# Retention and banded attention on one Trainium2 core: a gate tile moved inside a head's score blocks, and gate tiles one attention unit sooner

## The reference, cut to what matters

```
q_r, k_r, v_r, g_r, q_a, k_a, v_a, gate_r, gate_a = parts
y_r = retention_branch(q_r, k_r, v_r, g_r, ...) @ w_ret_o     # 8 heads, 64-wide keys, 128-wide values
y_a = attention_branch(q_a, k_a, v_a, ...) @ w_att_o          # 8 heads, band of 128 tokens to each side
mix = (sigmoid(gate_r) * y_r + sigmoid(gate_a) * y_a) @ w_mix_o
```

## Time and profile before

| | |
|---|---|
| median of 3 runs | 4184.95 us (4178.0 to 4199.9) |
| the profiled execution, own time | 4187.68 us |
| its span, first to last instruction | 4185.9 us |
| mean granted clock of TensorE | 0.973 |
| retention stage, layer 0 | about 184 to 345 us |
| attention stage, layer 0 | about 345 to 590 us |
| retention stage, layer 1 | about 1255 to 1412 us |
| attention stage, layer 1 | about 1412 to 1600 us |

### The profile page before, as it was taken

How to read it: one execution, slowest core, us unless ns; L and a number is a source line. 1 busy time by engine, 2 the same in 40 slices (tenths; PEclk the granted TensorE clock), 3 DMA queues, 4 the chain that set the end, 5 groups by cost and what they waited for, 6 DMA issues and landing times. The chain is left out here.

```text
span 4185.9 us, 55886 instructions
## 1 busy us (share of the span) xinstructions
PE 3987.6 (95%) x22458; PEld 3463.1 (83%) x22458; DVE 2238.5 (53%) x3931; ACT 1471.3 (35%) x2120; POOL 838.9 (20%) x763
## 2 busy tenths in 40 slices
PE   8999998999799999899979989899999999999998
PEld 7877798999684567888757887689999998999997
DVE  4333446445433344555547544347997665656664
ACT  3144345222313433522237343333333333333332
POOL 1000013111100001211101430006655563111100
PEclk9999999999998999999989999999999999999999
DMA  3101123222120112322212112226766777887873
GB/s 131 51 31 41 46 86 106 91 86 95 47 71 25 41 50 76 118 101 90 97 46 82 35 57 81 76 91 194 227 198 190 242 254 257 291 266 262 266 246 122
DMA packets 232448, 519.43 MB, mean 124 GB/s; under 512 B 36160, under 2 KB 134592, under 8 KB 231808
## 3 DMA queue, kind: packets, MB, share of 16 engines
q1 hardware_dynamic: 160752, 400.75, 29.1%
q0 software_dynamic: 18432, 67.12, 4.6%
q10 hardware_dynamic: 53008, 47.99, 3.4%
HBM read 454.66 MB, written 60.82 MB: 123 GB/s over the span
## 5 line engine op out<-in xcount | busy, mean ns | idle before, releaser
L304 PE MATMUL PSM<-UX,PARTS 128*128 128x264 f32 (+3 forms) x3392 | 1192.2, 351 | 43.0 <-DVE UX L333 26.3
L305 PE MATMUL PSM<-UX,PARTS 128*128 128x264 f32 (+3 forms) x3392 | 1171.9, 345 | 0.0
L306 PE MATMUL PSM<-UX,PARTS 128*128 128x264 f32 (+3 forms) x3392 | 1168.1, 344 | 0.0
L272 DVE TENSOR_TENSOR PARTS<-RAW,PARTS 128x1024 fp32r<-128x1024 f32 x549 | 687.3, 1258 | 627.1 <-ACT PARTS L262 627.0
L262 ACT ACTIVATE PARTS<-RAW 128x1024 fp32r<-128x1024 f32 x612 | 644.8, 1056 | 991.5 <-PE PSM L306 487.6
L304 PEld LDWEIGHTS PSM<-UX,PARTS 128*128 128x128 f32 x3392 | 651.2, 192 | 133.8 <-DVE UX L333 35.9
L305 PEld LDWEIGHTS PSM<-UX,PARTS 128*128 128x128 f32 x3392 | 651.9, 192 | 60.2 <-issue 3.1
L306 PEld LDWEIGHTS PSM<-UX,PARTS 128*128 128x128 f32 x3392 | 650.8, 192 | 59.7
L2543 PE MATMUL PSM<-AC,PARTS 128*128 128x448 f32 x1024 | 375.3, 367 | 3.8 <-DVE AC L2790 3.8
L2545 PE MATMUL PSM<-AC,PARTS 128*128 128x448 f32 x1024 | 374.6, 366 | 0.0
L2544 PE MATMUL PSM<-AC,PARTS 128*128 128x448 f32 x1024 | 374.6, 366 | 0.0
(11 more groups left out here) (378 smaller groups left out, 5747.5 us busy)
## 6 DMA issues: line engine op xcount, KB each, us to landing
RAW<-w_ff_dram SPq DMA_DIRECT2D x128, 512.0 KB, 3.5
RAW<-peer_u_dram SPq DMA_DIRECT2D x128, 512.0 KB, 4.0
RAW<-peer_v_dram SPq DMA_DIRECT2D x128, 512.0 KB, 4.5
RAW<-w_in_dram SPq DMA_DIRECT2D x116, 512.0 KB, 3.5
acts_dram<-MQ ACTq DMA_DIRECT2D x128, 224.0 KB, 4.2
MQ<-acts_dram SPq DMA_DIRECT2D x128, 224.0 KB, 3.5
MQ<-gates_dram SPq DMA_DIRECT2D x128, 224.0 KB, 4.3
RAW<-w_mix_o_dram SPq DMA_DIRECT2D x32, 512.0 KB, 3.5
```

Of the source, the lines that this page charges most:

```text
L272: e.tensor_tensor(p[:, 1024:2048], self.raw.of(i), p[:, 0:1024].bitcast(F), SUB).then_inc(V.sem, V.tick("w", i))
L304: e.matmul(dst, wh[k], xh_[k][:, lo:hi], start=(k == 0), stop=False, skip_group_check=True)
L305: e.matmul(dst, wh[k], xl_[k][:, lo:hi], start=False, stop=False, skip_group_check=True)
L306: m = e.matmul(dst, wl[k], xh_[k][:, lo:hi], start=False, stop=(k == kk - 1), skip_group_check=True)
```

## The change

In retention, the gate tile of turns 2 to 7 moves from behind all five score blocks to behind the third one, in both layers. Turns 8 and 9, which have no scores, are as before. In the attention of layer 0, gate tile f is written at turn 1 + 5f/2 instead of 2 + 5f/2, on PE, ACT and DVE alike, since all three ask `fill_at`. Nothing is added or removed, and `ret_act` and `ret_dve` keep their order.

```
             for h in range(10):
                 if h < 8:
                     for j, (j0, nj) in enumerate(JT):
...
                         gemm(e, b, [k_], [q_], n, rows=nj).then_inc(T.sem, T.tick("score", l, h, j))
-                if h >= 2:
-                    i = first["fill", l] + h - 2
-                    tile_pe(e, ("g", l, h - 2), i, W.both(i), us(c0, n), n)
+                        if h >= 2 and j == 2:
+                            gate(h - 2)
+                if h >= 8:
+                    gate(h - 2)
...
-            return [f for f in range(14) if u == (2 + f * 5 // 2 if l == 0 else 1 + 2 * f)]
+            return [f for f in range(14) if u == (1 + f * 5 // 2 if l == 0 else 1 + 2 * f)]
```

More of the change, by code:

```diff
@@ L608, in ret_pe, with gate @@
             e.wait_ge(V.sem, V.at("end", ("in", l)))
+            def gate(g):
+                i = first["fill", l] + g
+                tile_pe(e, ("g", l, g), i, W.both(i), us(c0, n), n)
             for h in range(10):
```

## The result

The changed kernel is slower: 4220.11 us median of 6 runs (4216.97 to 4229.67) against 4184.04 us, ratio 1.0081 with a 95% interval of 1.0066 to 1.0097, so 34 us, with 28 to 41 by the interval. I had forecast 4191 and no measurable change; the range ended at 4205. The profiled execution took 4229.67 us.

| stage | before | after | difference |
|---|---|---|---|
| retention, layer 0 | 164.3 | 161.7 | -2.6 |
| attention, layer 0 | 198.8 | 228.0 | +29.2 |
| retention, layer 1 | 161.3 | 166.2 | +4.9 |
| attention, layer 1 | 185.2 | 183.7 | -1.5 |
| all behind layer 1's mixing | 2471.8 | 2484.2 | +12.4 |

A forecast was written before the change was run, and what follows sets the result against it. PE was taken to bound the kernel, busy 95%. Retention +1.2, clock losses +7 and attention -2.5 gave +5.7 us: 4193.4 on the profiled time, 4191 from the median, no measurable change, range 4178 to 4205.

The forecast's parts named there:

- the attention's part: Layer 0's attention: first gate tile fills idle time, other tiles give nothing; gain 2.5 us, ends 0 and 7.5.
- The other 13 tiles: Layer 0's attention, gate tiles after the first: shift by one unit of about 2.5 us, counted as nothing either way.
- the clock in retention: Both retention stages before the change: 9.5 us in layer 0 and about 12.5 in layer 1, together 22, hang on the clock.
- The old wait on the tile: Retention: PE's wait for DVE's L724 isn't removed but moves from the fourth score block to the gate tile, about 1.1 us.
- the new wait on Silu: Retention: the variance sums wait for the gate tile's slot until ACT's Silu, about 1.9 us a turn, 2.8 in turn 2.
- The turn of 20.56: Layer 0's retention: period of a steady turn in the changed order at full clock, against 20.47 us before.
- Retention's sum: Both retention stages: +1.2 us without clock losses (+1.9 in layer 0, -0.7 in layer 1), and +7 us for the clock.
- The 7 us: Retention clock losses that stay: 0.55 us for each of ten turns, a third of the bound, and 0.7 for each turn 2.
- The attention's start: Start of layer 0's attention: first gate tile runs in the 7.49 us idle, second starts about 361.1; gain 2.5 us.
- The rival on the slower side: Retention: the clock falls at both waits, 2.3 us in each of ten turns, no attention gain; 4210 us, chance 0.09.

The follow-up runs named there:

- r_j1: `r_silu` with the retention gate tile behind a head's second score block instead of the third; 4157.41 us, ratio 0.9931 to the kernel before.
- r_only: The changed kernel with only retention's edit, attention's gate tiles standing as in the kernel before; 4196.69 us, ratio 1.0015 to the kernel before.
- r_silu: `r_only` with ACT's weight tile and Silu put ahead of the exponential of the next head's decays; 4178.42 us, ratio 0.9976 to the kernel before.
- a_bound: Kernel before with attention's edit alone, but the tiles of turns 11, 21 and 31 back at 12, 22 and 32; 4205.57 us, ratio 1.0038.

## Why the prediction was wrong

**The step that failed** is the last but one of the attention's part: "The other 13 tiles only shift by one unit of about 2.5 us inside a PE that has nearly no other idle there, so I give them nothing either way; were their cover worse, it would show as waits of L798, of which each can be some tenths of a us." They cost 32 us. The waits that I bounded by tenths are 1.2 us each, and these three are 3.5 us. The rest is the clock, for which that sentence has no term. I had weighed the clock only in retention, although the rule I used there (a short wait among matmuls that fill 64 rows) was in sight. What I hadn't done is to ask, of each tile moved, which wait it covered where it stood: the hand-over of a pair of heads was in the code, in `heads_out`, and the trace of before shows it covered.

The prediction had said that it would be wrong if the shifted tiles exposed waits in each unit. They did so only at the three hand-overs, and for 0.53 us two turns later, and this was enough.

**What bounds the kernel, and the clock in retention**: right. The 22 us that it laid to the clock are 25 by the windows of turns 2 to 7, and `r_j1` gives 28 back, clock and waits together.

**The old wait on the tile, the new wait on Silu**: right in place, and nearly in size: 1.80 us against 1.9, 0.82 against 1.1, 2.7 and 2.9 in turn 2 against 2.8. The turn of 20.56 is 20.5 and layer 1's 20.1 is 20.1, where the clock stays up.

**Retention's sum**: +1.2 and +7 for the clock, 8 us; measured with `r_only` +6 (0 to 13). Right, and so was the reason, in that the clock fell in some turns of 22 us and not in others. The 7 us were a third of a bound, an estimate between wide ends; in the trace of `r_only` the turns are longer than 20.5 and 20.1 us by 1.5 us in layer 0 and 6.8 in layer 1 (23.5, 22.1, 20.8, 20.8 and 20.1), 8.3 together. That it came so near is in part luck.

**The rule of the Trainium skill** (TensorE: Matmul & The Clock Gate, section Why this matters for your kernels), which warns only of long idle gaps between bursts: the runs speak against it as a sufficient rule. `r_silu`'s tile at 245.97 had 1.28 us of gap ahead of it and ran at 0.54; the last units of the changed kernel had no gap to speak of and ran at 0.51 for 31 us. What the Trainium skill says on the same page (section A second HAM failure mode: psum-queue depth-cycling), of short stops between groups of matmuls that cycle through PSUM buffers and make the clock swing, agrees with the place that decided, three waits of 1.2 us for a place in PSUM. I had named it for the slower rival, in another stage.

**The attention's start**: -2.5 forecast with 0 as one end, measured 0.9997, not told apart from either. The chain went as written: the second tile starts at 358.0, which with the stage's start 3.0 us earlier is the 361.1 of the text, and unit 3's scores wait 2.1 us for ACT's copy of the first.

**The rival on the slower side** had the right sign, some three quarters of the size (4210 is 25 us above the 4185 that it starts from, 34 were measured) and the wrong stage: it laid the loss on ten turns of retention. The chance of 0.07 for slower came from retention alone.

## What to carry to other kernels

Before filler work is moved, ask of each piece which wait of others it covers where it stands, above all at the rare turns (a hand-over, a first and a last unit) and not only in the steady state. On a ring of PSUM slots a move changes who waits for whom four takes later; if the reader's engine then has the reading behind something that depends on the moved work, reorder that engine too. And a wait of PE is to be priced with the clock behind it: here 3.5 us of new waits, with the short units beside them, became 32.

## What the runs showed of the hardware that I had not expected

TensorE can be busy without a break and stay at 1.2 GHz: from 529.4 to 556.8 in the changed kernel it is busy for 27.37 of 27.4 us at a granted clock of 0.50, in score products that fill 64 rows, transposes, and value products that fill 64 columns. The same units ran at 1.00 before, when they were entered at 1.00. Such work mostly kept whichever of the two levels it found, and where the clock fell behind a wait of 0.53 us, the low stretch lasted 10 to 31 us. It ended inside a gate tile in all cases but one, the stretch of 20.4 us in `a_bound`. A fall needs no wait: `r_j1` had two behind half-height blocks without a gap. And a fall can recur turn after turn: in `r_silu` turns of 18.9 us became 20.46 us in layer 0, and turns of 18.4 us became 20.0 in layer 1, each with one low stretch on the tile. Before the change layer 0's were 20.47 us, with one low stretch each, and without the wait they are 17.56.
